# Three gate slabs kept in SBUF, a ring of three places instead of four, finished rows formed in place

## What is computed

```python
x = x + (ga * branch_a + gb * branch_b) @ w_out
# _peer: 8 heads, 16 experts each, chosen per row by two halves of the query
u = jnp.take(u_tab, eidx, axis=0)
act = jax.nn.gelu(jnp.einsum('thkd,td->thk', u, xb), approximate=False)
coef = (g * act.astype(jnp.float32)).astype(xb.dtype)
return jnp.einsum('thk,thkd->td', coef, jnp.take(v_tab, eidx, axis=0))
```

## Time and profile before

| | us |
|---|---|
| median of 3 runs | 3385.7 (3383.65 to 3389.47) |
| the profiled execution | 3382.3 |
| its span, first to last instruction | 3380.2 |
| TensorE busy | 3112.7 (92%) |
| VectorE busy | 2423.6 (72%) |
| GpSimd busy | 1423.0 (42%) |
| ScalarE busy | 1220.3 (36%) |

### The profile page before, as it was taken

One profiled execution on the slowest core, in us unless ns is written; L12 is line 12 of the kernel. 1 busy time (PEld: TensorE's weight loads), 2 busy tenths in 40 slices (PEclk: granted clock), 3 DMA queues, 4 the chain that ended last, 5 costly groups with the idle time before them and its releaser, 6 DMA issues.

```text
span 3380.2 us, 33356 instructions
## 1 busy us (share of the span) xinstructions
PE 3112.7 (92%) x10016; PEld 1781.6 (53%) x10016; DVE 2423.6 (72%) x5476; ACT 1220.3 (36%) x4064; POOL 1423.0 (42%) x1244
## 2 busy tenths in 40 slices
PE   8999999999999999999999999999999777777776
PEld 6877565555555565655554665655554222322232
DVE  8827898666678798665678798665688666666664
ACT  4223443343334443343334444333333333233332
POOL 1202355343334455343434454343334555455453
PEclk9999999999999999999999999999999999999999
DMA  4357999999999999999999999999999999999998
GB/s 138 107 186 299 380 410 418 419 418 419 416 410 417 409 409 417 417 415 416 408 411 419 404 416 418 407 418 419 415 411 385 420 420 420 404 420 420 419 411 331
DMA packets 209604, 1311.20 MB, mean 388 GB/s; under 512 B 23632, under 2 KB 28880, under 8 KB 70160
## 3 DMA queue, kind: packets, MB, share of 16 engines
q0 software_dynamic: 156672, 1140.92, 82.2%
q1 hardware_dynamic: 51472, 167.36, 13.1%
q10 hardware_dynamic: 1280, 0.79, 0.1%
HBM read 1298.34 MB, written 10.64 MB: 387 GB/s over the span
## 4 chain that ended last, share of the span: by engine, by line
PE 63%; DMA 21%; DVE 9%; issue 3%; ACT 3%; POOL 1%; POOLq 0%; DVEq 0%; SPq 0%; ACTq 0%
PE ps_acc L784 35%; DMA rows<-in_experts,idx 21%; PE ps_a L596 16%; PE ps_v L596 4%; PE ps_a L686 4%; DVE rows L1468 4%; PE ps_a L713 1%; DVE va L1302 1%; ACT coef L953 1%; PE ps_y L653 1%; PE ps_a L690 1%; ACT diag L957 1%; POOL rows L1647 1%; PE ps_v L635 0%; PE ps_v L697 0%
## 5 line engine op out<-in xcount | busy, mean ns | idle before, releaser
L784 PE MATMUL ps_acc<-rows,diag 128*128 128x512 f32 x4352 | 1996.9, 608 | 232.3 <-ACT diag L957 231.0
L1647 POOL DMA_INDIRECT rows<-in_experts,idx x1088 | 1297.2, 1192 | 1693.8 <-PE ps_acc L784 1427.9
L1468 DVE CUSTOM_DVE_ANT_0 rows<-rows,xn 128x1024 f32<-128x1024 f32 x1088 | 1324.8, 1231 | 750.4 <-DMA rows<-in_experts,idx 732.3
L784 PEld LDWEIGHTS ps_acc<-rows,diag 128*128 128x128 f32 x4352 | 818.8, 193 | 1261.5 <-issue 868.0
L950 ACT ACTIVATE act_v<-dots 128x2 f32<-128x2 f32 x544 | 110.5, 203 | 1735.9 <-DVE dots L1468 1727.5
L957 ACT ACTIVATE diag<-pk,coef 128x128 f32<-128x128 f32 x1088 | 377.3, 394 | 17.7
L596 PE MATMUL ps_a<-xnT,ring 128*128 128x272 f32 x1536 | 369.8, 395 | 0.9 <-issue 0.8
L596 PEld LDWEIGHTS ps_a<-xnT,ring 128*128 128x128 f32 x1536 | 292.9, 191 | 91.1 <-issue 34.0
L953 ACT ACTIVATE coef<-act_v,soft 128x1 f32<-128x1 f32 x1088 | 261.4, 287 | 17.8
L1302 DVE SCALAR_TENSOR_TENSOR va<-va,pk 128x302 f32<-128x302 f32 x480 | 261.2, 607 | 0.5
L596 PE MATMUL ps_a<-gates,ring 128*128 128x272 f32 x1024 | 246.3, 394 | 2.5 <-ACT sig L924 1.7
(11 more groups left out here) (268 smaller groups left out, 1994.6 us busy)
## 6 DMA issues: line engine op xcount, KB each, us to landing
ring<-in_slabs SPq DMA_DIRECT2D x256, 512.0 KB
rows<-in_experts,idx POOLq DMA_INDIRECT x1088
ring<-made_slabs SPq DMA_DIRECT2D x24, 512.0 KB
xt<-in_x_prompt SPq DMA_DIRECT2D x4, 1024.0 KB, 13.2
out_y_prompt<-yt SPq DMA_DIRECT2D x8, 512.0 KB, 8.6
ring<-made_slabs SPq DMA_DIRECT2D x12, 256.0 KB
made_slabs<-rows SPq DMA_DIRECT2D x1, 2048.0 KB, 9.6
made_slabs<-rows SPq DMA_DIRECT2D x4, 512.0 KB, 9.2
```

The source lines that it names most:

```text
L784: ins = pe.matmul(ps_acc[:, h, :], diag[:, slot, :], rows[:, slot, D + h * 512:D + (h + 1) * 512], start=first, stop=False, skip_group_che ...
L1468: ins = dve.tensor_tensor_reduce(rows[:, slot, 0:D], rows[:, slot, 0:D], xn[:, :], 1.0, 0.0, ALU.mult, ALU.add, dots[:, s:s + 1])
L1647: pool.indirect_dma_start(out=rows[:, slot, :], out_offset=None, in_=experts, in_offset=bass.IndirectOffsetOnAxis(ap=idx[:, a, k:k + 1], a ...
```

## The change

The slabs of `gate` 7, 8 and 9 get a buffer of their own, `held`, which is loaded once, after the first ring loads. Their pieces take no part in the ring any more, in any group. `SLOTS` becomes 3. The room comes from `yt`, from one place of the ring and from `fold`: `end` and `end_scale` work in place in `x2t`, the store reads `x2t`, ScalarE's waste goes to `uS` or `xnT`, and `fold` is loaded late into a part of `gates`. Waits follow: the next rows enter `x2t` after the store has landed (`y_out`) rather than after the squares, `end` waits for no store, the load of the sample rows waits for the store of tile 6, and ScalarE waits for `fold_in` once. The rest of the diff passes the slab itself instead of its place's number.

```diff
-SLOTS = 4
+SLOTS = 3
 S_CONV, S_GATE, S_GLU, S_COUT, S_OUT, S_Q = 4, 12, 28, 36, 40, 48
+HELD = (S_GATE + 7, S_GATE + 8, S_GATE + 9)
...
+def row_of(piece, j):
+
+    return SLAB_OF[piece] + (2 * j if piece in ("cq", "cp") else j)
+
+
 def slabs_of(piece, j, streamed):
 
     if piece in SLAB_OF:
-        return (("given", SLAB_OF[piece] + (2 * j if piece in ("cq", "cp") else j)),)
+        row = row_of(piece, j)
+        return () if row in HELD else (("given", row),)
...
-        ("conv_b", CT), ("ln_g", CT), ("ln_b", CT), ("cache", CT * HALO), ("eye", P), ("fold", P),
-        ("iota", TOPK), ("keys", 2 * KEYS)]
+        ("conv_b", CT), ("ln_g", CT), ("ln_b", CT), ("cache", CT * HALO), ("eye", P),
+        ("iota", TOPK), ("keys", 2 * KEYS), ("fold", P)]
...
-        pk = sb("pk", [P, KEPT_W])
+        pk = sb("pk", [P, KEPT_W - P])
...
         ring = sb("ring", [P, SLOTS, D])
+        held = sb("held", [P, len(HELD), D])
...
+        fold = flat(outT)[:, 0:P]
...
-        yt = sb("yt", [P, D])
+        spent = [flat(uS)[:, 0:D], flat(xnT[:, :, :])[:, 0:D]]
...
-                sp.dma_start(y_t[t], yt[:, :]).then_inc(y_out, 16)
+                sp.dma_start(y_t[t], x2t[:, t % 2, :]).then_inc(y_out, 16)
...
-            sp.dma_start(pk[:, :], kept).then_inc(kept_in, 16)
+            sp.dma_start(pk[:, :], kept[:, 0:KEPT_W - P]).then_inc(kept_in, 16)
...
+            for i, row in enumerate(HELD):
+                sp.dma_start(held[:, i, :], slabs[row]).then_inc(held_in, 16)
...
-                    sp.wait_ge(y_sq, TILES - 1)
+                    sp.wait_ge(y_out, 16 * TILES)
...
+                    sp.dma_start(fold, kept[:, KEPT_W - P:KEPT_W]).then_inc(fold_in, 16)
...
-            sp.dma_start(y_sample.rearrange("b p d -> (b p) d"), yt[0:DEC, :]).then_inc(y_out, 16)
+            sp.dma_start(y_sample.rearrange("b p d -> (b p) d"), x2t[0:DEC, TILES % 2, :]).then_inc(y_out, 16)
...
             def slab(piece, j, g):
 
+                if piece in SLAB_OF and row_of(piece, j) in HELD:
+                    pe.wait_ge(held_in, 16 * len(HELD))
+                    return held[:, HELD.index(row_of(piece, j)), :]
                 n = slab_base(g) + plan(g).slab[piece, j]
                 pe.wait_ge(slab_in[n % SLOTS], 16 * (n // SLOTS + 1))
-                return n % SLOTS
+                return ring[:, n % SLOTS, :]
...
-                shape = par("fold") if n >= TILES * TPAIRS else par("eye")
+                shape = fold if n >= TILES * TPAIRS else par("eye")
                 cols = slice(b * BATCH, (b + 1) * BATCH)
+                if n == TILES * TPAIRS and b == 0:
+                    act.wait_ge(fold_in, 16)
...
-                act.activation(x2t[:, t % 2, :], yt[:, :], ACT.Square, accum_out=fin[:, 0:1]).then_inc(y_sq, 1)
+                act.activation(spent[t % 2 if t < TILES - 2 else 1], x2t[:, t % 2, :], ACT.Square, accum_out=fin[:, 0:1]).then_inc(y_sq, 1)
...
-                        dve.wait_ge(y_sq, 2 * g - 1)
+                        dve.wait_ge(y_out, 32 * g)
...
-                        dve.wait_ge(y_sq, 2 * g)
+                        dve.wait_ge(y_out, 16 * (2 * g + 1))
...
-                dve.wait_ge(y_out, 16 * t + 16)
                 dve.wait_ge(slot_free, RING + steps)
-                dve.tensor_tensor(yt[:, :], flat(ps_acc[:, :, :]), x2t[:, t % 2, :], ALU.add).then_inc(y_sum, 1)
+                dve.tensor_tensor(x2t[:, t % 2, :], flat(ps_acc[:, :, :]), x2t[:, t % 2, :], ALU.add).then_inc(y_sum, 1)
...
+                if t == 0:
+                    dve.wait_ge(y_out, 16)
                 dve.wait_ge(y_std, t + 1)
-                dve.scalar_tensor_tensor(yt[:, :], yt[:, :], fin[:, 2:3], gl[:, :], ALU.mult, ALU.mult).then_inc(y_ready, 1)
+                dve.scalar_tensor_tensor(x2t[:, t % 2, :], x2t[:, t % 2, :], fin[:, 2:3], gl[:, :], ALU.mult, ALU.mult).then_inc(y_ready, 1)
...
```

More of the change, by code:

```diff
@@ L315, in program @@
         norms_in = sem("norms_in")
+        fold_in = sem("fold_in")
         slab_in = [sem(f"slab_in{i}") for i in range(SLOTS)]
+        held_in = sem("held_in")
         made_stored = sem("made_stored")
@@ L560, in _ @@
             sp.wait_ge(x_in, 32 * GROUPS)
+            sp.wait_ge(held_in, 16 * len(HELD))
         @block.tensor
@@ L589, in second_slab, with product @@
                 return n % SLOTS
-            def product(out, slot, k0, rhs):
+            def product(out, weights, k0, rhs):
                 kt = rhs.shape[1]
                 for k in range(kt):
-                    w = ring[:, slot, (k0 + k) * P:(k0 + k + 1) * P]
+                    w = weights[:, (k0 + k) * P:(k0 + k + 1) * P]
                     last = pe.matmul(out[:, 0:N], w, rhs[:, k, :], start=(k == 0), stop=(k == kt - 1))
@@ L629, in states @@
                 else:
-                    slot = slab("s", t, g)
+                    weights = slab("s", t, g)
                 for c in range(2):
@@ L633, in states @@
                     for i in range(CT):
-                        w = ring[:, slot, (2 * i + c) * P:(2 * i + c + 1) * P] if g else wb[:, 4 * t + i, c, :]
+                        w = weights[:, (2 * i + c) * P:(2 * i + c + 1) * P] if g else wb[:, 4 * t + i, c, :]
                         last = pe.matmul(out[:, i * NK:(i + 1) * NK], w, uS[:, t, i * NK:(i + 1) * NK], start=True, stop=True)
@@ L644, in outputs @@
                 else:
-                    slot = slab("y", t, g)
+                    weights = slab("y", t, g)
                     second = second_slab("y", t, g)
@@ L651, in outputs @@
                     for c in range(2):
-                        w = ring[:, slot, (2 * i + c) * P:(2 * i + c + 1) * P] if g else wc[:, j, c, W32:]
+                        w = weights[:, (2 * i + c) * P:(2 * i + c + 1) * P] if g else wc[:, j, c, W32:]
                         last = pe.matmul(out, w, hst[:, t % 2, c, i, 0:NK], start=False, stop=(c == 1))
@@ L681, in out_slab @@
             def out_slab(j, g):
-                out, slot = a_tile(a_at(g, "out", j)), slab("out", j, g)
+                out, weights = a_tile(a_at(g, "out", j)), slab("out", j, g)
                 pe.wait_ge(x_in, 32 * (g + 1))
                 for k in range(DT):
-                    last = pe.matmul(out[:, 0:N], ring[:, slot, k * P:(k + 1) * P], merged[:, k, :],
+                    last = pe.matmul(out[:, 0:N], weights[:, k * P:(k + 1) * P], merged[:, k, :],
                                      start=(k == 0), stop=(k == DT - 1))
```

## The result

| | before | after |
|---|---|---|
| median | 3385.5 us (10 runs) | 3395.93 us (10 runs, 3390.86 to 3397.41) |
| the profiled execution | 3382.3 us | 3396.7 us |
| its span | 3380.2 us | 3394.5 us |
| moved | 1311.20 MB | 1306.48 MB |

The change makes the kernel slower by 0.3%: the ratio is 1.0028, with an interval of 1.0020 to 1.0036. The forecast was 3385.7, no change.

A forecast was written before the change was run, and what follows sets the result against it. TensorE and full DMA transfers stand close together as bounds in groups 1 to 3. Opening +4.6, groups -4.8 and the extra `fold` DMA +0.2 sum to 0.0 us, so 3385.7 us, range 3375 to 3398.

The forecast's parts named there:

- The opening's wait: Opening: the slab of `out` 3 is issued behind SyncE's stores, so TensorE waits; +4.6 us, bounds 0 and 5.7.
- The wait at `y` 1: Groups 1 to 3: second slab of `y` 1 lands late on three places; stall 2.4 us, between 1.3 and 6.5.
- What arrives of the saved bytes: Groups 1 to 3: stall and saving together give -2.0, -2.0 and -0.8 us, sum -4.8.
- the bound of -11.3: Groups 1 to 3: largest gain, the transfers' saving of 3.75 us arriving in full in each group.
- in group 3 nothing is in reserve: Group 3, between two waiting places: at 304 GB/s transfers can't get ahead of TensorE, so only -0.8 us.
- The idleness near 590 is gone; that near 780 stays in part: Group 1, profile after: TensorE's first idle place, 2.86 us, vanishes; the second, 4.44 us, remains partly.
- The steps that cost nothing: Rows in place: additions, squares and scalings keep shapes and counts, 0; new store waits covered by turns in between.
- `u` 2, `gate` 4 and `gate` 6: Groups 1 to 3, next tight ring loads: `u` 2 hidden by 0.7 us; at 11.5 us landings each costs 2.1.
- `gate` 0's 0.2 us: Groups 1 to 3, behind `y` 1: slab lands at 500.4, needed at 500.2, adding 0.2 us to the stall.
- The first gather: End of the opening: starts near 286.5 us instead of 281.9.
- The rival named *Slower: Groups 1 to 3: the `y` 1 stall isn't given back, each group costs 2.6 us; 3398.3 us, chance 0.20.
- The other rival: Whole launch: queue reserve holds in all groups, opening's wait hidden; 0.2 - 11.3 = -11.1, 3374.6 us, chance 0.22.

The follow-up runs named there:

- the version with the wait filled: Changed kernel plus six overwritten products ahead of `y` 1 in groups 1 to 3, so TensorE isn't idle there; 3384.40 us, 0.9992 of before.
- the version with nothing held: Changed kernel with `SLOTS = 4` and `HELD = ()`, keeping rows in place, the squares' waste elsewhere and `fold` late; 3387.16 us, 1.0001 of before.
- the ring of three alone: Kernel before with `SLOTS` 3 instead of 4 and nothing else, no loads saved; 3402.15 us, 1.0041 of before.
- both costs removed: Changed kernel with SyncE's six opening stores spread one a half and six overwritten products ahead of `y` 1; 3378.35 us, 0.9976 of before.

## Why the prediction was wrong

**The two waits: place and length right, price too low.** The opening's wait was forecast at +4.6; it came as a pause of 5.60 us and then a clock of 0.69:

```profile
232.00:240.00 8.00, 7.47 (x26) 6.09 (x27) 0.00 (x0) 0.47 (x2) 0.00 (x0) 0.69 0.27 109
```

That is +6.7 from `out` 0 to `out` 5, and +5.6 to +6.5 up to turn 0 (1.0 more against the second profile of before). The working followed only the slab's landing and then counted the next product at its old 4.6 us; it took 6.8. The wait at `y` 1 was forecast at 2.4 us and is 2.20 to 2.3. The load that nobody could see before, 256 KB alone, was put at 7.4 us; in after's chain of group 1 it takes 7.20:

```profile
497.66 0.02 issue
497.68 7.20 DMA ring<-made_slabs
504.88 0.14 issue
```

But the launch's three stretches with `y` 1 grew by 20.5 us in all (19.1 in the second profile), not by 3 x 2.6 = 7.8. That is the step that failed: "I take 7.4 ... The stall is 2.4 us" priced a stall by its length. The products behind it run at 1.2 GHz for a while, and the version with the wait filled shows what of it remains at the end of the groups: 10.4 us, 3.5 for each `y` 1. The rows to see it were there: the earlier trace rows have a clock of 0.96 and 0.95 in the windows where TensorE idles for 4.44 and 3.36 us. The text used these rows for the idleness and passed over the clock beside it. Cut finer, the window of 30 us in group 3 of before has it in one place:

```profile
2080.00:2085.00 5.00, 3.70 (x10) 1.43 (x8) 4.75 (x13) 3.90 (x8) 1.59 (x2) 1.00 1.01 419
2085.00:2090.00 5.00, 2.94 (x4) 1.39 (x5) 4.96 (x11) 1.75 (x6) 0.49 (x1) 0.69 1.02 422
```

The Trainium skill ("TensorE: Matmul & The Clock Gate", HAM oscillation — how this bites in real kernels) describes a case of this kind: a block of matmuls is shorter than the wait for the DMA behind it, and TensorE drops to half its clock in every such tile. The trace agrees as to the drop, which came at `out` 3 and at `y` 1 of each group. It differs as to the case: ahead of the wait of 2.20 us at 505.02 the engine had been busy without a pause since 490 us or earlier.

**What arrives of the saved bytes: about right, for a wrong reason.** -4.8 was forecast for the groups with the waits in it, +2.4 came; without the lost clock it is -8.0. So apart from the clock the groups gain more than was forecast, and the bound of -11.3 holds. The argument that in group 3 nothing is in reserve (the dip to 304 GB/s) stays open. With the wait filled, turns 12 to 76, 76 to 140 and 140 to 200 gain 3.7, 1.7 and 2.6 us, so the last is not behind the others; but with nothing saved and the wait filled it gains 2.6 as well, while the first gains nothing and the second loses 2.0. The parts scatter too much to tell what the bytes give in one group. "The idleness near 590 is gone; that near 780 stays in part" holds: in after TensorE idles for 0.81 of the 25 us from 585, and for 3.14 of the 40 us from 770.

```profile
585.00:610.00 25.00, 24.19 (x78) 14.44 (x77) 19.77 (x44) 11.36 (x35) 9.74 (x10) 1.00 1.02 418
770.00:810.00 40.00, 36.86 (x107) 19.55 (x106) 28.31 (x64) 13.38 (x42) 16.99 (x16) 1.00 1.01 418
```

**The steps that cost nothing.** Rows in place, the squares, the new waits for the store's landing: confirmed within 0.1% by the version with nothing held, but for the later `out` 0 that the new start may cause. `u` 2, `gate` 4 and `gate` 6 don't wait. `gate` 0's 0.2 us doesn't show. The first gather was expected at 286.5 us and starts at 293.93: 12.0 after that of before, of which 5.3 are the later `out` 0 and 6.7 the wait at `out` 3 with what follows.

**The sum.** Forecast +4.6 - 4.8 + 0.2 = 0.0. Measured in the profiles behind `out` 0: +5.6 and +6.5 (opening), +2.4 twice (groups), +0.9 and +0.4 (turns alone; all profiles scatter from -0.3 to +1.7 here), so +9.0 and +9.4, and the medians say +10.4 and +7.3. The term of the groups carries 7.2 of it, that of the opening 1 to 2.

**The rivals.** The rival named *Slower* gave 3398.3, near the measured time, but by luck: its mechanism isn't what happened. It said that the wait is not given back because the gathers come later too. The waits for `diag` shrank by 12.6 us, and by 6.4 in the ring of three alone, where its waits at `y` 1 are 7.0 and nothing is saved; so most of the wait was given back. The clock took it away again. The other rival, a full gain of 11.3, is what the transfers could give, and with both costs removed 7.6 of it arrives.

## What to carry to other kernels

Price a stall of TensorE with the time behind it: look at the granted clock in the windows where the engine already idles. Here stalls of 2.2 to 2.3 us cost 5.7 to 7.4 us in after, where the clock fell behind them, and one of 1.7 us cost 2.0 where it did not. Before a ring is made shallower, list for each load what SyncE has queued ahead of it; here moving six stores was worth about as much as the whole change cost. A saving and its price should be measured apart: nine loads fewer were worth 7 to 8 us all along, hidden under 10 us of lost clock.

## What was not expected of the hardware

An idle time of 2.2 us between small products was enough to bring the granted clock down to 0.50 over the 5 us that follow:

```profile
1254.24 0.67 PE L668 MATMUL ps_y<-uy,ring 128*128 128x68 f32 x2 [2.24 <-DMA ring<-made_slabs]
...
1259.39 6.15 PE L802 MATMUL ps_acc<-rows,diag 128*128 128x512 f32 x8
```
```profile
1255.00:1260.00 5.00, 5.00 (x23) 4.83 (x23) 4.79 (x13) 0.36 (x2) 0.00 (x0) 0.50 1.02 415
1260.00:1265.00 5.00, 5.00 (x8) 1.93 (x7) 5.00 (x11) 4.52 (x20) 1.08 (x1) 0.56 0.99 405
```

The clock fell behind all twelve waits at `y` 1 in the four profiles that have them (2.17 to 2.50 us). Length alone does not decide it: before waits for `diag` 34 times in groups 1 to 3, up to 4.0 us, and its clock falls in eight places there.

Six products without use, 2.97 us of work in each group, made the changed kernel 10 us faster.
